# Expert layers of a two-block transformer: from gathering each token's experts to multiplying with all experts on TensorE

## The chip, the cores and the metric

The kernel runs on one core of a Trainium2 chip. The metric is the time of the device for one execution, in microseconds (us), as the median of several runs.

## What is computed

The program is two blocks on 256 tokens of width 1024. The change touches only `peer`, the expert layer. It is called three times on 256 tokens: in layer 0 for the latent tokens and for the context tokens, in layer 1 for the latent tokens.

```python
PEER_HEADS = 8; PEER_N_KEYS = 128; PEER_TOPK = 16        # 128 * 128 = 16384 experts
qry = (xb @ w_query).reshape(P, 8, 2, 128)
s = einsum('phcd,hckd->phck', qry, sub_keys)             # two scores of 128 keys for each head
top_s, top_i = top_k(s, 16)
cand_s = top_s[..., 0, :, None] + top_s[..., 1, None, :] # 256 candidates
best_s, pos = top_k(cand_s, 16)
idx = take_along_axis(top_i0 * 128 + top_i1, pos)        # 16 experts for each token and head
gate = softmax(best_s)
act = gelu(einsum('pd,phkd->phk', xb, u_tab[idx]))
return einsum('phk,phkd->pd', gate * act, v_tab[idx])
```

So each token takes 8 x 16 = 128 of 16384 experts. U and V have 16384 rows of 1024 numbers each, 67 MB a table and a layer in f32.

## The kernel before

The program is a list of stages (`Begin`, `Ada`, `DeltaNet`, `Peer` for layer 0, `Attention`, `Peer` for layer 1, and eight more). Each stage writes out one instruction list for each engine, and each engine starts a stage when all engines have ended the one before. SyncE (SP) alone runs ahead: it only issues loads into a ring of three buffers of 1 MB (`Ring.load`), and each load waits until the matmuls that read the block three loads earlier have ended.

`Peer` works on tiles of 128 tokens, four in layer 0 (stage `peer_a`) and two in layer 1 (`peer_m`). A tile's tokens lie on the 128 partitions. The steps are these.

- `NormFirst` normalizes the tiles and turns them into `hT`. `pe_step` projects queries and scores them against the keys, job by job.
- For each unit, a tile and a head, `dve_choose` picks the 16 experts of each token: MAX8, FIND_INDEX8 and MATCH_REPLACE8 over 128, 128 and 256 values, then a comparison with a row of numbers (`iota`) that turns positions into keys.
- For each of the unit's 16 experts per token, `pool_rows` (L1859) gathers by an indirect DMA one row of U and V together, 8 KB for each token, 1 MB for 128 tokens, into one of 8 buffers. A buffer is gathered into again when the matmul of 8 gathers before has ended.
- `dve_dot` (L1901) multiplies the U half with the token and sums it. ScalarE takes the gelu (L1794), `dve_coef` (L1913) multiplies with the gate, ScalarE makes a diagonal matrix of the 128 coefficients (L1801), and TensorE multiplies it with the V half into PSUM (`pe_sum`, L1766: two matmuls of 512 columns).

There are 32 units in layer 0 and 16 in layer 1, so 768 gathers of 1 MB, and as many rounds of these steps.

## Time and profile before

| | |
|---|---|
| time of three runs | 4365.11, 4366.67, 4370.96 us, median 4366.67 |
| span of the profiled execution | 4368.7 us |
| expert stage of layer 0 | 1196.8 to 2574.1 us |
| expert stage of layer 1 | 2724.5 to 3432.0 us |
| TensorE matmul busy over the span | 85% |
| VectorE, ScalarE, GpSimd busy | 58%, 22%, 28% |
| data moved | 1043.56 MB, mean 239 GB/s |

The profiled execution's own time is one of the three, which isn't named; the three lie from 3.6 us below to 2.3 us above its span. The span runs from the first instruction to the last. The stages follow one another on all engines, so the length of a stage adds to the time in full. Within a stage the engines overlap, and what counts is the step that the others wait for. TensorE's busy time holds waits inside its pipeline.

### The profile page before, as it was taken

What the parts mean: (1) busy time and instruction counts of PE and PEld (TensorE: products, weight loads), DVE (VectorE), ACT (ScalarE), POOL (GpSimd) and SP (SyncE); (2) the same over time, 40 slices, a digit from 0 to 9 for tenths busy, and PEclk for the clock granted to TensorE, in tenths of its full rate; (3) what the DMA queues carried; (4) which work ended last, traced back from release to release, by engine and by line L of the source; (5) the groups of instructions that cost most, each with busy time, mean ns of one, the idle gap of its engine ahead of it and who ended that gap; (6) DMA issues with size and microseconds to landing.
All of it is one profiled execution on the core that took longest, in us unless ns stands there. A gap on an engine that the chain in (4) does not pass through costs nothing.

```text
span 4368.7 us, 60065 instructions
## 1 busy us (share of the span) xinstructions
PE 3704.5 (85%) x23239; PEld 2027.7 (46%) x23239; DVE 2515.1 (58%) x5831; ACT 966.5 (22%) x2602; POOL 1218.9 (28%) x1241
## 2 busy tenths in 40 slices
PE   6898899888989987777777789888777789899999
PEld 2456744576444433222322235543222358546674
DVE  1345733567266777777777645767776347636341
ACT  0233312232132222222222212222222121010100
POOL 1004400243023444444444410344444100006000
PEclk7798999899999999999999999999999999999999
DMA  9410012100289999999999952999999524330443
GB/s 378 162 59 4 4 58 68 40 4 3 91 323 399 418 416 420 418 413 410 414 414 407 420 227 66 363 416 418 418 413 419 188 81 135 121 120 11 148 145 125
DMA packets 269482, 1043.56 MB, mean 239 GB/s; under 512 B 19394, under 2 KB 103596, under 8 KB 170896
## 3 DMA queue, kind: packets, MB, share of 16 engines
q0 software_dynamic: 114736, 815.52, 45.8%
q1 hardware_dynamic: 154464, 224.18, 15.3%
...
## 4 chain that ended last, share of the span: by engine, by line
PE 49%; DMA 27%; DVE 12%; ACT 4%; issue 4%; POOL 3%; DVEq 0%; POOLq 0%; ACTq 0%
DMA arena<-in_peer_uv,arena 25%; PE psum L261 13%; PE psum L1766 11%; PE psum L299 4%; PE psum L749 4%; PE psum L1724 3%; PE psum L788 3%; DVE arena L1901 2%; DMA arena<-in_ada_w 2%; PE psum L212 2%; POOL arena L1859 1%; PE psum L1091 1%; ACT arena L1801 1%; PE psum L1102 1%; DVE arena L946 1%
## 5 line engine op out<-in xcount | busy, mean ns | idle before, releaser
L1766 PE MATMUL psum<-arena 128*128 128x512 f32 x3072 | 1460.0, 620 | 392.4 <-ACT arena L1801 387.8
L1901 DVE SCALAR_TENSOR_TENSOR arena<-arena 128x1024 bf16<-128x1024 f32 x768 | 940.9, 1225 | 522.2 <-DMA arena<-in_peer_uv,arena 491.9
L1859 POOL DMA_INDIRECT arena<-in_peer_uv,arena x768 | 864.4, 1125 | 1174.1 <-PE psum L1766 1035.8
L1766 PEld LDWEIGHTS psum<-arena 128*128 128x128 f32 x3072 | 574.6, 196 | 1228.2 <-ACT arena L1801 636.8
L261 PE MATMUL psum<-ring,arena 128*128 128x512 f32 (+2 forms) x1408 | 593.1, 585 | 25.4 <-DVE arena L2780 9.1
L261 PEld LDWEIGHTS psum<-ring,arena 128*128 128x128 f32 x1408 | 269.3, 199 | 342.8 <-issue 316.5
L1794 ACT ACTIVATE arena<-arena 128x2 f32<-128x2 f32 x384 | 78.3, 204 | 1243.1 <-DVE arena L1901 1243.0
L1801 ACT ACTIVATE arena<-consts,arena 128x128 f32<-128x128 f32 x768 | 268.3, 394 | 224.6 <-DVE arena L1913 221.4
L299 PE MATMUL psum<-arena,ring 128*128 128x256 f32 x1408 | 309.6, 381 | 9.8 <-DVE arena L2775 7.7
L299 PEld LDWEIGHTS psum<-arena,ring 128*128 128x128 f32 x1408 | 267.3, 191 | 50.2 <-issue 6.4
L749 PE MATMUL psum<-arena,ring 128*128 128x512 f32 x512 | 230.4, 605 | 1.6 <-issue 1.6
L1724 PE MATMUL psum<-arena,ring 128*128 128x128 f32 (+3 forms) x704 | 181.7, 409 | 8.9 <-ACT arena L1539 8.9
L212 PE MATMUL psum<-consts,arena 128*128 128x128 f32 (+3 forms) x705 | 104.1, 290 | 67.3 <-DMA arena<-in_ev_b_spatial 19.1
L1724 PEld LDWEIGHTS psum<-arena,ring 128*128 128x128 f32 x704 | 119.7, 199 | 77.4 <-issue 49.5
L749 PEld LDWEIGHTS psum<-arena,ring 128*128 128x128 f32 x512 | 97.2, 195 | 113.8 <-issue 113.8
L212 PEld LDWEIGHTS psum<-consts,arena 128*128 128x128 f32 (+3 forms) x705 | 85.2, 149 | 115.2 <-issue 44.4
L2963 POOL TENSOR_TENSOR arena<-arena 128x512 f32<-128x512 f32 x32 | 40.6, 1269 | 331.2 <-DVE arena L2998 331.2
L330 ACT ACTIVATE arena<-x_res 128x1024 f32<-128x1024 f32 x10 | 10.6, 1060 | 486.0 <-DVE x_res L2787 322.0
L1298 POOL MEMSET arena<- 128x512 f32 x8 | 4.2, 522 | 391.8 <-ACT arena L902 391.7
L788 PE MATMUL psum<-ring,arena 128*128 128x512 f32 x256 | 110.4, 593 | 1.6 <-ACT arena L885 1.6
L1913 DVE SCALAR_TENSOR_TENSOR arena<-arena 128x2 f32<-128x2 f32 x384 | 81.1, 211 | 32.8 <-ACT arena L1794 31.4
L946 DVE SCALAR_TENSOR_TENSOR arena<-arena 128x512 f32<-128x512 f32 x128 | 96.2, 752 | 4.6
...
## 6 DMA issues: line engine op xcount, KB each, us to landing
arena<-in_ada_w SPq DMA_DIRECT2D x48, 1024.0 KB, 14.6
ring<-in_ffn_w_up SPq DMA_DIRECT2D x44, 1024.0 KB, 5.1
ring<-in_dn_w_in SPq DMA_DIRECT2D x24, 1024.0 KB, 5.3
ring<-in_peer_w_query SPq DMA_DIRECT2D x22, 1024.0 KB, 7.1
ring<-in_ffn_w_down SPq DMA_DIRECT2D x20, 1024.0 KB, 5.0
arena<-in_peer_uv,arena POOLq DMA_INDIRECT x768, 12.8
ring<-in_ev_w_in SPq DMA_DIRECT2D x10, 1024.0 KB, 5.2
ring<-in_dn_w_out SPq DMA_DIRECT2D x8, 1024.0 KB, 4.9
```

What stands on the lines that cost most here:

```text
L212: return e.transpose(out, in_, self.k.const("ident")[0:n, 0:n])
L261: m = e.matmul(o, self.hT[:, k0 + k, t * 128:(t + 1) * 128], w[:, k, :], start=k0 + k == 0, stop=k0 + k == self.KC - 1)
L299: m = e.matmul(self.bank(c)[:, 0:self.nt], w[:, k, j * 128:(j + 1) * 128], self.hT[:, k, 0:self.nt], start=k == 0, stop=k == self.KC - 1)
L749: m = e.matmul(k.banks[j % 4], w[:, q, j % 2 * 128:(j % 2 + 1) * 128], self.hT[:, q, :], start=q == 0, stop=q == 7)
L788: m = e.matmul(k.banks[t * 2 + nh], self.oT[:, k0 + q, t * 128:(t + 1) * 128], w[:, q, nh * 512:(nh + 1) * 512], start=k0 + q == 0, stop=k ...
L946: e.scalar_tensor_tensor(acc, p[:, :, w:w + 256], self.cw[:, c, w:w + 1], acc, MUL, ADD).then_inc(*V.up(("conv", half, j)))
L1724: m = e.matmul(k.banks[j % 2][:, 0:w_], w[:, n, c % 2 * 128:(c % 2 + 1) * 128], self.hT[:, n, a * 128:b * 128], start=n == 0, stop=n == 7)
L1766: m = e.matmul(k.banks[4 + t % 2 * 2 + nh], self.diag[g % self.ND], self.vsl[g % self.NS][:, nh * 512:(nh + 1) * 512], start=u % 8 == 0 an ...
L1801: e.activation(self.diag[g % self.ND], k.const("ident"), ACT.Copy, bias=0.0, scale=self.cf[u % 2][:, s:s + 1]).then_inc(*S.up(("dg", g)))
L1859: e.indirect_dma_start(self.uv[g % self.NS], None, self.table(), bass.IndirectOffsetOnAxis(ap=self.eid[u % 6][:, s:s + 1], axis=0)).then_i ...
L1901: e.scalar_tensor_tensor(self.junk[g % 2], self.us[g % self.NS], 1.0, self.h[:, u // 8, :], MUL, MUL, accum_out=self.a[u % 2][:, s:s + 1]) ...
L1913: e.scalar_tensor_tensor(self.cf[u % 2][:, c], self.lg[u % 4][:, c], self.sm[u % 4], self.ge[u % 2][:, c], MUL, MUL,).then_inc(*V.up(("cf" ...
```

## The change

The gathers are gone. Every expert is worked out for every token, and those that a token didn't choose get a gate of zero. 256 tokens (two tiles) make a half: layer 0 has two halves (`self.halves`), layer 1 has one. U and V are given in another layout (`peer_ut`, `peer_vt`), so that a load of 1 MB holds 256 experts, 8 KB for each partition, and lands in the ring of three buffers.

- `pe_u(n, c)`: chunk c of 128 experts, half n: 8 matmuls of 256 columns, experts on the partitions of PSUM and tokens in the columns. ScalarE's gelu puts the result into `Xs[:, c, :]`, which holds 128 chunks x 256 tokens for each partition, 128 KB.
- `pe_v(n, c)`: the same chunk's part of the output: 4 matmuls of 512 columns, with `Xs[:, c, :]` as weights.
- Order on TensorE: all of U of half 0 (128 chunks), then V of half n - 1 and U of half n chunk by chunk in turn (layer 0 only), then all of V of the last half.
- The gates: for a token, the 128 pairs (key 0, key 1) with their gates, turned so that pairs lie on partitions. A group is 4 tokens. VectorE compares keys with `iota` (`dve_group`, 128 x 1024), GpSimd multiplies one half with the gates (`pool_group`, 128 x 512, in place), TensorE multiplies the two (4 matmuls of 128 x 128), which gives the 128 x 128 gates of each of the 4 tokens. There are 64 groups for each half, and two buffers `hot`. They lie on TensorE in 66 slots behind the U chunks of a half (64 groups and two turns): chunks 60 to 120 of half 0 in layer 0, 76 to 120 in layer 1, 64 to 121 of half 1.
- ScalarE copies a group out of PSUM, and after each fourth writes 1 MB to DRAM (`G_d`, pieces of 512 bytes), from two buffers in turn: 16 writes a half. SP reads it back in 16 loads of 1 MB into one buffer `Gb`, one for 8 chunks. VectorE multiplies it into `Xs` (`dve_coef`, 128 x 2048), and `pe_v` of the 8 chunks waits for that.
- The choice of the experts (`dve_unit`, 16 for each half) stays, in one piece for each unit. `Norm` takes the place of `NormFirst`, and each query job is 8 matmuls over all tiles at once (`pe_query`, 16 jobs; `pe_score`).

The core of the diff:

```diff
+        self.Xs = flat.rearrange("p (c t) -> p c t", c=128)
+        self.stg = [res[:, 0:2048], res[:, 2048:4096] if nt > 2 else k.al(2048)]
+        self.Gb = hT[:, 0:2048]
+        self.hot = [k.al3(2, 4, 128) for _ in range(2)]
+        self.G_d = [k.nc.dram_tensor(f"coef_{name}_{n}", [16, 128, 256, 8], F32, kind="Internal").ap() for n in range(self.halves)]
...
+    def span(self, n):
+        if n:
+            return 64, 122
+        return (60, 121) if self.nt > 2 else (76, 121)
+    def slots(self, n, c):
+        a, b = self.span(n)
+        upto = lambda c: min(self.LAST, max(0, (c - a + 1) * self.LAST // (b - a)))
+        return range(upto(c - 1), upto(c)) if c else range(upto(0))
+    def exps(self, n):
+        if n:
+            return {30: 0, 60: 1}
+        return {20: 0, 58: 1} if self.nt > 2 else {34: 0, 72: 1}
...
 def sp(self, e):
...
+        for j in range(0, 16, 2):
+            load_block(k, e, self.query_key(j), k.i["peer_w_query"][l], 0, 8, j * 128, 256)
+        for b in range(64):
+            self.sp_rows(e, "u", 0, b)
+        for n in range(self.halves):
+            for b in range(64):
+                self.sp_rows(e, "v", n, b)
+                if b == 0:
+                    self.sp_coef(e, n, 0)
+                elif b % 4 == 1 and b < 60:
+                    self.sp_coef(e, n, b // 4 + 1)
+                if n + 1 < self.halves:
+                    self.sp_rows(e, "u", n + 1, b)
+    def sp_rows(self, e, kind, n, b):
+        table = self.k.i["peer_ut" if kind == "u" else "peer_vt"]
+        self.k.ring.load(e, (self.name, kind, n, b), lambda a: a, table[self.l, b])
+    def sp_coef(self, e, n, b):
+        if b == 0:
+            for s in (14, 15):
+                e.wait_ge(*self.l_put[s % 2].at(("put", n, s)))
+            e.wait_ge(*(self.V.at(("coef", n - 1, 15)) if n else self.P.at(("u", 0, 127))))
+        else:
+            e.wait_ge(*self.V.at(("coef", n, b - 1)))
+        e.dma_start(self.Gb, self.G_d[n][b].rearrange("j t i -> j (t i)")).then_inc(*self.l_got.up(("got", n, b)))
...
+        for n in range(self.halves + 1):
+            for c in range(128):
+                if n:
+                    self.pe_v(e, n - 1, c)
+                if n < self.halves:
+                    self.pe_u(e, n, c)
+                    for s in self.slots(n, c):
+                        self.pe_slot(e, n, s)
+    def pe_u(self, e, n, c):
+        ring, key = self.k.ring, self.u_key(n, c)
+        if c % 2 == 0:
+            e.wait_ge(*ring.ready(key))
+        if c >= 2:
+            e.wait_ge(*self.S.at(("ge", n, c - 2)))
+        elif n:
+            e.wait_ge(*self.S.at(("ge", n - 1, 126 + c)))
+        w = ring.buf(key).rearrange("p (c k m) -> p c k m", c=2, k=8)
+        for q in range(8):
+            m = e.matmul(self.k.banks[4 + c % 2][:, 0:256], w[:, c % 2, q, :], self.hT[:, n, q, :], start=q == 0, stop=q == 7)
+        m.then_inc(*self.P.up(("u", n, c)))
+        if c % 2:
+            ring.free(key, self.P)
+    def pe_v(self, e, n, c):
+        k, ring, key = self.k, self.k.ring, self.v_key(n, c)
+        if c % 2 == 0:
+            e.wait_ge(*ring.ready(key))
+        if c % 8 == 0:
+            e.wait_ge(*self.V.at(("coef", n, c // 8)))
+        if c == 0:
+            if n == 0:
+                e.wait_ge(*self.S.at(("sc", 15)))
+            else:
+                e.wait_ge(*self.S.at(("ge", n, 127)))
+                e.wait_ge(*self.S.at(("ev", n, 63)))
+        w = ring.buf(key).rearrange("p (c d) -> p c d", c=2)
+        for t in range(2):
+            for nh in range(2):
+                m = e.matmul(self.y_bank(n, t, nh), self.Xs[:, c, t * 128:(t + 1) * 128], w[:, c % 2, nh * 512:(nh + 1) * 512],
+                             start=c == 0, stop=c == 127)
+        m.then_inc(*self.P.up(("v", n, c)))
+        if c % 2:
+            ring.free(key, self.P)
...
+    def pe_slot(self, e, n, s):
+        P, b = self.P, self.slot_bank(s)
+        if s >= 2:
+            e.wait_ge(*self.taken(n, s - 2))
+        elif n:
+            e.wait_ge(*self.taken(n - 1, self.LAST - 2 + s))
+        if s in self.TURNS:
+            t = self.TURNS.index(s)
+            e.wait_ge(*self.V.at(("gate", n, t)))
+            for w in range(3):
+                m = self.turn(e, b[:, w * 128:(w + 1) * 128], self.PK[t][:, w, :])
+            m.then_inc(*P.up(("tp", n, t)))
             return
+        g = self.group(s)
+        e.wait_ge(*self.G.at(("gated", n, g)))
+        rows, cols = self.hot[g % 2][:, 1], self.hot[g % 2][:, 0]
+        for q in range(4):
+            m = e.matmul(b[:, q * 128:(q + 1) * 128], rows[:, q, :], cols[:, q, :], start=True, stop=True)
+        m.then_inc(*P.up(("g", n, g)))
...
+        if self.nt > 2:
+            e.wait_ge(*self.l_x.at("x"))
+        for n in range(self.halves):
+            for c in range(128):
+                if n == 0 and c == self.free_at[0]:
+                    e.wait_ge(*V.at(("picked", 0, 15)))
+                if n == 0 and c == self.free_at[1]:
+                    e.wait_ge(*self.l_sc.at("s"))
+                e.wait_ge(*P.at(("u", n, c)))
+                e.activation(self.Xs[:, c, :], k.banks[4 + c % 2][:, 0:256], ACT.Gelu, bias=0.0, scale=1.0).then_inc(*S.up(("ge", n, c)))
+                if c in self.exps(n):
+                    self.act_exp(e, n, self.exps(n)[c])
+                for s in self.slots(n, c):
+                    if s not in self.TURNS:
+                        self.act_group(e, n, self.group(s))
...
+    def act_group(self, e, n, g):
+        S, s = self.S, g // 4
+        lane, stg = self.l_put[s % 2], self.stg[s % 2].rearrange("p (b t i) -> p b t i", b=16, t=16)
+        if g % 4 == 0 and (s >= 2 or n):
+            e.wait_ge(*lane.at(("put", n, s - 2) if s >= 2 else ("put", n - 1, 14 + s)))
+        e.wait_ge(*self.P.at(("g", n, g)))
+        slot = g + 1 + (g > 1)
+        e.activation(stg[:, :, g % 4 * 4:g % 4 * 4 + 4, :].rearrange("p b t i -> p t b i"),
+                     self.slot_bank(slot).rearrange("p (t b i) -> p t b i", t=4, b=16), ACT.Copy, bias=0.0, scale=1.0).then_inc(*S.up(("ev", n, g)))
+        if g % 4 == 3:
+            e.wait_ge(*S.now())
+            e.dma_start(self.G_d[n][:, :, 16 * s:16 * s + 16, :].rearrange("b j t i -> j b (t i)"),
+                        stg.rearrange("p b t i -> p b (t i)")).then_inc(*lane.up(("put", n, s)))
...
+    def pool_group(self, e, n, g):
+        rows = self.hot[g % 2][:, 1]
+        e.wait_ge(*self.V.at(("hot", n, g)))
+        e.tensor_tensor(rows, rows, self.PT[g // 32][:, 2, g % 32 * 4:g % 32 * 4 + 4].unsqueeze(2).to_broadcast([128, 4, 128]),
+                        MUL).then_inc(*self.G.up(("gated", n, g)))
...
+        for u in range(16):
+            self.dve_unit(e, 0, u)
+        self.dve_first(e, 0)
+        for g in range(4, 64):
+            self.dve_group(e, 0, g)
+        for n in range(1, self.halves):
+            self.dve_coef(e, n - 1, 0)
+            for b in range(16):
+                if b < 15:
+                    self.dve_coef(e, n - 1, b + 1)
+                if b < 8:
+                    for u in (2 * b, 2 * b + 1):
+                        self.dve_unit(e, n, u)
+                else:
+                    if b == 8:
+                        self.dve_first(e, n)
+                    for g in range(max(4, 9 * (b - 8)), min(64, 9 * (b - 7))):
+                        self.dve_group(e, n, g)
+        last = self.halves - 1
+        for b in range(16):
+            self.dve_coef(e, last, b)
+            if b == 5:
+                for n in range(last):
+                    self.dve_add(e, n)
+        self.dve_add(e, last)
+    def dve_first(self, e, n):
+        self.dve_turned(e, n, 0)
+        self.dve_group(e, n, 0)
+        self.dve_group(e, n, 1)
+        self.dve_gates(e, n, 1)
+        self.dve_group(e, n, 2)
+        self.dve_group(e, n, 3)
+        self.dve_turned(e, n, 1)
...
+    def dve_group(self, e, n, g):
+        V, P = self.V, self.P
+        if g < 4 or g == 32:
...
+        e.tensor_tensor(self.hot[g % 2], self.k.const("iota").unsqueeze(1).unsqueeze(1).to_broadcast([128, 2, 4, 128]),
+                        self.PT[g // 32][:, 0:2, g % 32 * 4:g % 32 * 4 + 4].unsqueeze(3).to_broadcast([128, 2, 4, 128]),
+                        ALU.is_equal).then_inc(*V.up(("hot", n, g)))
+    def dve_coef(self, e, n, b):
+        e.wait_ge(*self.l_got.at(("got", n, b)))
+        e.wait_ge(*self.S.at(("ge", n, 8 * b + 7)))
+        x = self.Xs[:, 8 * b:8 * b + 8, :]
+        e.tensor_tensor(x, x, self.Gb.rearrange("p (t i) -> p i t", i=8), MUL).then_inc(*self.V.up(("coef", n, b)))
...
-    given["peer_uv"] = np.concatenate([given.pop("peer_u"), given.pop("peer_v")], axis=2)
+    u = given.pop("peer_u").reshape(2, 64, 2, 128, 8, 128).transpose(0, 1, 5, 2, 4, 3)
+    given["peer_ut"] = np.ascontiguousarray(u).reshape(2, 64, 128, 2048)
+    v = given.pop("peer_v").reshape(2, 64, 2, 128, 1024).transpose(0, 1, 3, 2, 4)
+    given["peer_vt"] = np.ascontiguousarray(v).reshape(2, 64, 128, 2048)
```

On TensorE, in the middle of a tile of layer 0, the order before was: two matmuls for a gather (its buffer's name is uv0, uv1, ...), each pair with a wait for the gather and for ScalarE, and projection steps between.

```order
L1766 MATMUL psum<-arena 128x512 [waits uv0_peer_a_landed,act_peer_a]
L1766 MATMUL psum<-arena 128x512
L1766 MATMUL psum<-arena 128x512 [waits uv1_peer_a_landed,act_peer_a]
L1766 MATMUL psum<-arena 128x512
L212 MATMUL psum<-consts,arena 128x128 x8
L1766 MATMUL psum<-arena 128x512 [waits uv2_peer_a_landed,act_peer_a]
L1766 MATMUL psum<-arena 128x512
L1724 MATMUL psum<-arena,ring 128x512 [waits act_peer_a,ring0_landed]
L1724 MATMUL psum<-arena,ring 128x512 x3
L1766 MATMUL psum<-arena 128x512 [waits uv3_peer_a_landed,act_peer_a]
L1766 MATMUL psum<-arena 128x512
L1766 MATMUL psum<-arena 128x512 [waits uv4_peer_a_landed,act_peer_a]
```

At the start of the stretch where both halves are worked on, TensorE's order now is this: L1721 is V of half 0, L1701 is U of half 1, and the ring's three buffers are named in the waits.

```order
L1721 MATMUL psum<-ring,arena 128x512 [waits act_peer_a,dve_peer_a,ring2_landed]
L1721 MATMUL psum<-ring,arena 128x512 x3
L1701 MATMUL psum<-arena,ring 128x256 [waits act_peer_a,ring0_landed]
L1701 MATMUL psum<-arena,ring 128x256 x7
L1721 MATMUL psum<-ring,arena 128x512 x4
L1701 MATMUL psum<-arena,ring 128x256 [waits act_peer_a]
L1701 MATMUL psum<-arena,ring 128x256 x7
L1721 MATMUL psum<-ring,arena 128x512 [waits ring1_landed]
L1721 MATMUL psum<-ring,arena 128x512 x3
L1701 MATMUL psum<-arena,ring 128x256 [waits act_peer_a,ring2_landed]
L1701 MATMUL psum<-arena,ring 128x256 x7
L1721 MATMUL psum<-ring,arena 128x512 x4
```

The waits for 768 gathers are gone, and a wait for one of three ring buffers stands ahead of every second V and every second U chunk. The U block of two chunks takes the buffer of the V block of the two chunks before (ring2 here), and that V block is in use until its last matmul.

On SP's queue the loads of layer 0 before were these: the queries, a row of gates for the end, and the next stage's weights.

```order
L104 DMA ring<-in_peer_w_query 128x8x256 [waits pe_dn] x2
L104 DMA ring<-in_peer_w_query 128x8x256 [waits pe_peer_a] x10
L1671 DMA arena<-gates_d 128x1024 [waits dve_peer_a]
L104 DMA ring<-in_att_w_in 128x4x512 [waits pe_peer_a] x3
L104 DMA ring<-in_att_w_in 128x4x512 [waits pe_att] x3
```

Now the same queue holds the U and V blocks, and the loads of the gates (L1632) among them.

```order
L104 DMA ring<-in_peer_w_query 128x8x256 [waits pe_peer_a] x6
L104 DMA ring<-in_peer_ut 128x2048 [waits pe_peer_a] x64
L104 DMA ring<-in_peer_vt 128x2048 [waits pe_peer_a]
L1632 DMA arena<-coef_peer_a 128x2048 [waits pe_peer_a,coef_out1_peer_a_landed,coef_out0_peer_a_landed]
L104 DMA ring<-in_peer_ut 128x2048 [waits pe_peer_a]
L104 DMA ring<-in_peer_vt 128x2048 [waits pe_peer_a]
L1632 DMA arena<-coef_peer_a 128x2048 [waits dve_peer_a]
L104 DMA ring<-in_peer_ut 128x2048 [waits pe_peer_a]
L104 DMA ring<-in_peer_vt 128x2048 [waits pe_peer_a]
L104 DMA ring<-in_peer_ut 128x2048 [waits pe_peer_a]
L104 DMA ring<-in_peer_vt 128x2048 [waits pe_peer_a]
L104 DMA ring<-in_peer_ut 128x2048 [waits pe_peer_a]
```

64 U blocks stand behind the queries, then V and U in turn, and each load of the gates waits for VectorE's multiplication of the one before.

## Rows read from the trace of the kernel before

**Rows 1.** The page: chain by line; a group, busy | idle before.

```profile
DMA arena<-in_peer_uv,arena 25%; PE psum L261 13%; PE psum L1766 11%; PE psum L299 4%; PE psum L749 4%; PE psum L1724 3%; PE psum L788 3%; DVE arena L1901 2%; DMA arena<-in_ada_w 2%; PE psum L212 2%; POOL arena L1859 1%; PE psum L1091 1%; ACT arena L1801 1%; PE psum L1102 1%; DVE arena L946 1%
...
L1766 PE MATMUL psum<-arena 128*128 128x512 f32 x3072 | 1460.0, 620 | 392.4 <-ACT arena L1801 387.8
```

**Rows 2.** Busy time by stretch: expert stages, then an FFN.

```profile
core 0: us, PE busy (x) PEld busy (x) DVE busy (x) ACT busy (x) POOL busy (x), PEclk, DMA share, GB/s
1196.80:1277.00 80.20, 60.60 (x300) 42.65 (x301) 53.16 (x158) 30.86 (x83) 20.02 (x18) 0.87 0.81 288
1277.00:2571.00 1294.00, 1040.77 (x2366) 434.64 (x2364) 915.28 (x2272) 326.06 (x904) 554.42 (x495) 0.98 1.00 410
2724.50:2767.00 42.50, 34.28 (x216) 30.59 (x216) 26.90 (x94) 17.25 (x41) 8.17 (x9) 0.96 0.80 289
2767.00:3429.00 662.00, 527.73 (x1264) 230.97 (x1264) 459.36 (x1139) 161.70 (x467) 282.83 (x248) 0.97 0.99 407
4090.00:4242.00 152.00, 151.99 (x704) 133.79 (x704) 73.94 (x151) 9.94 (x23) 0.00 (x0) 1.00 0.45 146
```

**Rows 3.** The chain in order of time: start us, length us.

```profile
632.69 55.22 PE psum L788 x128
1203.79 3.82 PE psum L1724 x32
4090.01 152.20 PE psum L299 x704
```

**Rows 4.** Loads: issues, size, median us from issue to landing.

```profile
ring<-in_ffn_w_up SPq DMA_DIRECT2D x44, 1024.0 KB, 5.1
ring<-in_peer_w_query SPq DMA_DIRECT2D x22, 1024.0 KB, 7.1
ring<-in_peer_sub_keys SPq DMA_DIRECT2D x2, 0.5 KB, 6.3
```

**Rows 5.** The loads of in_ffn_w_down, 20 of 24 with 1 MB.

```profile
DMA to landing us min/median/max: 3.5/5.0/5.5
```

**Rows 6.** Timeline of SP at 4104 us: start, length of the issue.

```profile
4104.10 0.37 SPq L104 DMA_DIRECT2D ring<-in_ffn_w_up  x1
```

**Rows 7.** Timeline of VectorE: starts of two units of the choice.

```profile
1208.80 0.30 DVE L1932 MAX8 arena<-arena 128x8 f32<-128x128 f32 x1 [3.25 <-ACT arena L1829]
...
1218.22 0.30 DVE L1932 MAX8 arena<-arena 128x8 f32<-128x128 f32 x1
```

**Rows 8.** Groups by shape on VectorE.

```profile
L955 DVE TENSOR_TENSOR arena<-arena 128x1024 f32<-128x1024 f32 x8 | 9.8, 1226 | 0.3
```

**Rows 9.** The page: a group on GpSimd.

```profile
L2963 POOL TENSOR_TENSOR arena<-arena 128x512 f32<-128x512 f32 x32 | 40.6, 1269 | 331.2 <-DVE arena L2998 331.2
```

**Rows 10.** Timeline of VectorE and GpSimd from 499.2 us.

```profile
499.20 0.82 POOL L1319 TENSOR_TENSOR arena<-arena 128x384 f32<-128x384 f32 x1
...
499.99 1.26 POOL L1321 TENSOR_TENSOR arena<-arena,consts 128x512 f32<-128x512 f32 x1
...
500.49 1.18 DVE L1448 TENSOR_TENSOR arena<-arena 128x384 f32<-128x384 f32 x1
...
501.21 1.13 POOL L1319 TENSOR_TENSOR arena<-arena 128x384 f32<-128x384 f32 x1
...
505.27 0.52 DVE L1448 TENSOR_TENSOR arena<-arena 128x384 f32<-128x384 f32 x1
```

**Rows 11.** Timeline of TensorE behind layer 0's experts.

```profile
2574.12 5.36 PE L212 MATMUL psum<-consts 128*128 128x128 f32 x24 [3.00 <-issue]
...
2587.36 5.13 PE L261 MATMUL psum<-ring,arena 128*128 128x512 f32 x8 [1.51 <-ACT arena L340]
```

**Rows 12.** Timeline: norm of four tiles, start and what follows.

```profile
146.16 1.06 ACT L330 ACTIVATE arena<-x_res 128x1024 f32<-128x1024 f32 x1 [124.25 <-DVE arena L572]
...
159.69 5.57 PE L261 MATMUL psum<-ring,arena 128*128 128x64 f32 x25 [0.84 <-ACT arena L340]
```

**Rows 13.** Timeline: norm of two tiles, its start.

```profile
4082.91 1.06 ACT L330 ACTIVATE arena<-x_res 128x1024 f32<-128x1024 f32 x1 [1.53 <-DVE x_res L3019]
```

539 lines of the change are left out of this document (177 added, 362 removed).

## Prediction

> **What bounds the kernel now.** I start with the stages. The two expert stages last 1377.3 us (1196.8 to 2574.1) and 707.5 us (2724.5 to 3432.0), 2084.8 of a span of 4368.7. Beside them only the loads that SP issues ahead of the next stage move, so the answer is the new length of these two. Next the busy times by stretch [rows 2]: in both stretches of gathers the DMA engines are busy for a share of 0.99 to 1.00 and move 407 to 410 GB/s. At that rate 1 MB (1.049 million bytes) takes 2.56 us, and 768 of them 1965. The chain agrees [rows 1]: 25% of it are gathers; TensorE's 11% in L1766 stand between them because a buffer comes free with its matmul. So DMA is the bound.
>
> How much of TensorE is in use there is the next question, and the busy row can't tell: 1041 of 1294 us hold waits inside the pipeline.
>
> **The price of a matmul.** It must be taken for each instruction of the program, not for each record. The kernel issues two matmuls for each of 768 gathers, 1536, and the page counts 3072 [rows 1]: a matmul in f32 leaves two records. An FFN layer shows the same: 22 blocks of 1 MB (44 loads for two layers [rows 4]), 16 matmuls each, are 352, and the chain counts 704 in 152.20 us [rows 3]. So:
> - 256 columns: 152.20 / 352 = 0.432 us. This is the very shape of U, from the same ring, with no stop.
> - 512 columns: 55.22 / 64 = 0.863 us, the shape of V (L788, 128 records).
> - 128 columns: 3.82 / 16 = 0.239 us. A turn leaves one record, 0.119.
>
> A U chunk is 8 x 0.432 = 3.46 us, a V chunk 4 x 0.863 = 3.45, a group of gates 4 x 0.239 = 0.955. TensorE's real work for the gathers before was 1536 x 0.863 = 1326 us of 1956, under the DMA's bound.
>
> The Trainium skill has two figures here. FP8 and Floating Point Precision, TensorE Precision Notes, says that true FP32 takes 4 passes through the array; Perfetto Trace Analysis, Engine Utilization, halves the peak output rate for FP32_LOW_HIGH. The trace sides with the first: 0.863 us for 512 columns are 2070 cycles at 2.4 GHz, 4.04 a column; the second fits only a single record. By the first the sum is as below, by the second TensorE's share of it is half (rival 3).
>
> **What the change removes.** All 1965 us of gathers, 768 sums on VectorE and as many diagonals. **What it adds:** three passes over U and V. On TensorE 3 x 128 x (3.46 + 3.45) = 2653 us, and 192 groups, 183. On DMA 3 x 128 loads of 1 MB, 48 writes and 48 reads of gates: 480 x 2.56 = 1229 us, or 1300 if the writes in 512-byte pieces cost 4.1 each (below). TensorE has more than twice the DMA's work, and more than the stages last now. It becomes the bound, if the others keep ahead of it.
>
> **Layer 0, step by step.**
> - Norm of four tiles: 13.5 us from its start to the next projection [rows 12].
> - Queries: 16 jobs of 8 x 0.863 + 4 x 0.239 = 7.86 us, 125.7. One us for the last score's copy, and 2 for a slow clock: behind a gap 8 records of 512 columns took 5.13 us, against 3.45 [rows 11, 3].
> - U of half 0: 128 x 3.46 = 442.8, 64 groups 61.1, turns 0.7: 504.6.
> - Turn to V: the first gates are loaded only behind the last U matmul, since `Gb` lies in `hT`. 0.25 us to SP's issue (two blocks from 4090.01 end at 4103.85 [rows 3], the issue is at 4104.10 [rows 6]), about 4.8 for the load (5.0 is the median [rows 5]; pieces of 8 KB instead of 2 and 4, so 0.2 off, an estimate), and a product of 128 x 2048, twice 1.23 [rows 8]: 7.5, with TensorE idle. Then the slow clock: 24 turns took 5.36 us, against 2.9 [rows 11]; 3 us. Sum 10.5.
> - V of half 0 and U of half 1: 128 x 6.91 = 884.5, groups 61.8: 946.3.
> - V of half 1: 441.7 and 0.8 for the last gelu: 442.5.
> - The sums at the end: 3.6 us as before.
>
> Sum: 13.5 + 128.7 + 504.6 + 10.5 + 946.3 + 442.5 + 3.6 = 2049.7, against 1377.3: **672.4 us more**.
>
> **Layer 1.** Norm of two tiles 8 (7.1 from 4082.91 to 4090.01 [rows 13, 3], and the keys' turns ahead), queries 16 x (3.46 + 0.48) + 1 = 64, U 504.6, turn 10.5, V 441.7, end 3.6. Sum 1032.4 against 707.5: **324.9 us more**.
>
> Together 997.3, and the span goes to 5366. The profiled execution lies 2 us over the median: **5364 us**.
>
> **What hides the rest, and with what margin.**
> - *The ring.* In the stretches of one kind a block lasts 6.92 us, and a load has two blocks' time. The thin place is the mixed stretch: the U block of 2b, 2b+1 goes into the buffer of the V block of 2b-2, 2b-1, free after V(2b-1). Until U(2b) TensorE has U(2b-1) and V(2b), 6.91 us, and the load takes 0.25 + 4.8 = 5.05. Without that cover each us of lateness costs 64. At 7.1, the landing of query blocks beside gathers [rows 4], it is 0.44 x 64 = 28 us.
> - *The groups.* The comparison takes 1.23 us [rows 8], the multiplication 1.27 [rows 9], and they don't overlap [rows 10]: VectorE's product of 128 x 384, 0.52 us alone, took 1.18 when it began at 500.49, and ended 0.42 behind GpSimd's (501.25); GpSimd's next took 1.13 behind it, not 0.82. So a group needs 2.5 us. TensorE asks for one each 4.1 us in layer 0 ((61 x 3.46 + 62) / 66), 3.3 in layer 1 (45 chunks), 7.0 in the mixed stretch (58). With no cover 64 x 2.5 would stand in each half, 480 in all.
> - *VectorE's choice.* A unit takes 9.4 us [rows 7], 16 take 151, and the first groups come 208 us (layer 0) and 263 us (layer 1) into U, behind 128 and 64 us of queries. The eleventh unit waits for an exponential that ScalarE issues at chunk 20 or 34 (69 and 118 us into U); six units behind it are 56 us, still in time. In the mixed stretch two units and a product are 21 us for 8 chunks of 55.
> - *The gates' writes.* A write takes some 4.1 us of DMA: 1 MB in 512-byte pieces lands after 6.3 us [rows 4], 1.5 over my 4.8. Four groups, its period, are 13 us or more. VectorE holds groups back at each eighth chunk of the mixed stretch, waiting for the next gates (about 7 us, then 2.5), but TensorE needs the first of them only 14.8 us in.
> - *ScalarE* has a gelu and a copy for each chunk, about 1 us of 3.46.
>
> **The unknown costs, from both sides.** Ring: 0 or 28. Turns, two of them: with a landing of 3.5 and no slow clock 4.3 less each, with 7.1 and twice the slow clock 5.3 more each; 10 either way. Groups: if the multiplication with its broadcast took twice as long, the pair needs 3.8 us, over layer 1's 3.3: 66 x 0.5 = 33 more. Writes: none of this kind stands in the trace. Free, nothing changes; at twice the price, 8.2, a period of 13 us still holds one and two loads (13.3), so nothing but some lateness changes; at thrice, 12.3, it lacks 4.4 us, 16 x 4.4 = 70 more in layer 1. Slots: 200 changes of shape on TensorE, nothing or 0.1 us each, 20. Clock: granted 1.00 in the FFN's 152 us, 0.98 in the gathers [rows 2]; at 0.98 throughout it is 2% of 3082, 60 more.
>
> **The rivals.**
> 1. *Slower still: TensorE is kept waiting.* Landings of 7.1, groups at 3.8, the clock at 0.98: 28 + 33 + 60, so 5390 to 5485. For it: such dense work for 2000 us isn't in the trace. Against it: the FFN asked the same ring for a block each 6.92 us, as the new stretches do, and ran without a stop. Chance 0.2.
> 2. *The gates' traffic stops ScalarE.* Gelus stand behind a copy that waits for a write; 48 writes each 10 us over their period would give 480 more, 5844. It begins at a write of 13 us in layer 1 and 16 in layer 0. Chance 0.04.
> 3. *Not slower: an f32 matmul costs one record.* If in these shapes the two records overlapped, a chunk were 1.73 us. TensorE's 3025 us of work in the stages (2653 + 183 + 189 of queries) halve, 1512 less; the ring then lacks 5.05 - 3.46 = 1.6 us for each pair in the mixed stretch, 102, and the pair of VectorE and GpSimd sets the pace of the groups, 25 and 53: 5366 - 1512 + 180 = 4034. It would have to hold for new instructions of just the shapes that cost two records in L299 and L788. The case turns when 997 of the 3025 go, at 67% of the rows' price. Chance 0.02.
> 4. *Somewhat less:* a V chunk uses each weight tile for two matmuls in a row, and the turns may be short: 10 to 35 us less, 5330 to 5350. Chance 0.06.
>
> **How the numbers follow.** My forecast, 5350 to 5390, has 0.66; the first rival 0.2, the second 0.04, the third 0.02, the fourth 0.06, and 0.02 for what I don't see, with either sign. The range of 5330 to 5460 takes in most of the first and the fourth. A measurement of this kernel can tell about 0.2%. Slower 0.97, same 0.005, faster 0.025.
>
> **What would show it.** TensorE's busy share in the new stages near 1 and its clock at 1.00; in the page 6144 records for U, 3072 for V and 1536 for groups; V alone at 3.45 us a chunk, a ring load that lands in 5 us and waits for TensorE, DMA share under 0.5, GpSimd's multiplications a chunk apart, two idle times of 7.5 us ahead of the first V. The prediction is wrong if the chain names DMA, ScalarE or GpSimd in these stages for more than some 30 us, or if a U chunk takes anything but 3.46.

## The result and the profile after

The changed kernel takes **5348.24 us** (median; 5345.55 to 5349.44) beside 4365.89 (4363.11 to 4370.96) for the kernel before on the same chip: a ratio of 1.224, with a 95% interval of 1.2226 to 1.2261. 5364 was forecast. The profiled execution has a span of 5347.5 us at a mean clock of 0.971.

The page, the chain by line and five groups (busy, mean ns | idle before, releaser), which answer to [rows 1]:

```profile
PE 84%; DVE 7%; ACT 3%; issue 3%; DMA 2%; POOL 2%; DVEq 0%; SPq 0%; POOLq 0%; ACTq 0%
PE psum L1721 25%; PE psum L1701 25%; PE psum L261 11%; PE psum L299 4%; PE psum L1757 3%; PE psum L1673 3%; PE psum L752 3%; PE psum L791 2%; DMA arena<-in_ada_w 2%; PE psum L212 1%; PE psum L1094 1%; PE psum L1105 1%; DVE arena L949 1%; POOL arena L2979 1%; POOL arena L2980 1%
...
L1701 PE MATMUL psum<-arena,ring 128*128 128x256 f32 x6144 | 1364.9, 379 | 0.0
L1721 PE MATMUL psum<-ring,arena 128*128 128x512 f32 x3072 | 1344.6, 594 | 18.4 <-issue 17.7
...
L1924 DVE TENSOR_TENSOR arena<-arena 128x2048 f32<-128x2048 f32 x48 | 186.3, 3881 | 1075.3 <-DMA arena<-coef_peer_a 644.0
...
L1915 DVE TENSOR_TENSOR arena<-consts,arena 128x1024 f32<-128x1024 f32 x192 | 232.3, 1224 | 603.9 <-PE psum L1757 603.8
L1851 POOL TENSOR_TENSOR arena<-arena 128x512 f32<-128x512 f32 x192 | 228.6, 1197 | 1426.2 <-DVE arena L1915 1426.2
```

TensorE now holds 84% of the chain, and U (L1701) and V (L1721) a quarter of the span each. In front of the 3072 matmuls of U TensorE never waited; in front of V 18.4 us, nearly all of it the two turns. The other engines wait for it or for each other: VectorE's comparison (L1915) for TensorE, GpSimd (L1851) for VectorE. In the page's list of loads the ring keeps pace:

```profile
ring<-in_peer_ut SPq DMA_DIRECT2D x192, 1024.0 KB, 4.8
ring<-in_peer_vt SPq DMA_DIRECT2D x192, 1024.0 KB, 4.8
...
coef_peer_a<-x_res ACTq DMA_DIRECT2D x32, 1024.0 KB, 5.8
arena<-coef_peer_a SPq DMA_DIRECT2D x32, 1024.0 KB, 6.9
```

Busy time by stretch of the changed kernel, layer 0 and then layer 1 (queries, U, turn, mixed, V), answers to [rows 2]:

```profile
1209.80:1335.80 126.00, 126.00 (x385) 63.85 (x386) 59.72 (x232) 18.62 (x32) 0.00 (x0) 0.99 0.19 60
1335.80:1836.40 500.60, 500.11 (x2566) 446.43 (x2565) 158.58 (x371) 94.50 (x199) 72.09 (x66) 1.00 0.50 170
1836.40:1845.30 8.90, 0.00 (x0) 0.01 (x1) 3.84 (x1) 0.38 (x1) 0.00 (x0) 0.76 0.87 345
1845.30:2789.80 944.50, 942.73 (x3590) 642.34 (x3590) 278.44 (x616) 92.99 (x198) 81.78 (x80) 1.00 0.51 179
2789.80:3229.60 439.80, 439.70 (x1024) 194.48 (x1024) 63.76 (x24) 0.00 (x0) 1.53 (x3) 1.00 0.53 196
...
3454.30:3954.70 500.40, 499.91 (x2567) 446.67 (x2566) 168.78 (x415) 94.32 (x199) 84.57 (x65) 1.00 0.50 167
3954.70:3963.90 9.20, 0.40 (x2) 0.03 (x1) 3.84 (x1) 0.38 (x1) 0.00 (x0) 0.64 0.59 228
3963.90:4408.00 444.10, 441.48 (x1024) 195.12 (x1024) 60.70 (x19) 0.00 (x0) 0.00 (x0) 1.00 0.52 188
```

The first figure behind the length is TensorE's busy time: 500.11 of 500.60, 942.73 of 944.50, 439.70 of 439.80, with a granted clock of 1.00. DMA, at 0.99 to 1.00 in the stretches of gathers before, is down at 0.50 to 0.53 in these long stretches. The bound moved from DMA to TensorE, whose work is simply longer. Layer 0's stage lasts 2039.3 us (1377.3 before), layer 1's 1027.9 (707.5): 982.4 more together, and the span grew by 978.8.

The timeline of the first turn shows what a turn is made of:

```profile
1834.73 1.67 PE L1701 MATMUL psum<-arena,ring 128*128 128x256 f32 x7
...
1836.50 0.33 SPq L1632 DMA_DIRECT2D arena<-coef_peer_a  x1
...
1841.38 3.84 DVE L1924 TENSOR_TENSOR arena<-arena 128x2048 f32<-128x2048 f32 x1 [33.13 <-DMA arena<-coef_peer_a]
...
1845.32 5.46 PE L1721 MATMUL psum<-ring,arena 128*128 128x512 f32 x6 [8.92 <-issue]
```

U's last matmul ends at 1836.40, the gates' load is issued 0.10 us later and has landed at 1841.38, the product takes 3.84, and V starts at 1845.32. Its first records are slow, as in [rows 11]: the chain has 6.60 us for 8 of them, where 4 x 0.863 = 3.45 is the full clock's price, and the granted clock is 0.50 from 1845.3 to 1851.0. Layer 1's turn is shorter in this part: 8.81 us idle, a granted clock of 0.50 only from 3963.9 to 3967.0, and 441.5 us for V where half 1 of layer 0 took 439.7 without a gap ahead of it.

### The profile page after: what moved, and what is told of

Its sections match the earlier page's. It is cut to its first block, busy times and chain, and to the rows that moved or that the text cites. A ratio compares the mean times of both kernels' runs of the same rounds, so it can differ in the third digit from the quotient of the medians.

```text
span 5347.5 us, 70742 instructions
## 1 busy us (share of the span) xinstructions
PE 5062.9 (95%) x30697; PEld 3344.0 (63%) x30697; DVE 1926.4 (36%) x4079; ACT 760.9 (14%) x1806; POOL 594.6 (11%) x685
## 4 chain that ended last, share of the span: by engine, by line
PE 84%; DVE 7%; ACT 3%; issue 3%; DMA 2%; POOL 2%; DVEq 0%; SPq 0%; POOLq 0%; ACTq 0%
PE psum L1721 25%; PE psum L1701 25%; PE psum L261 11%; PE psum L299 4%; PE psum L1757 3%; PE psum L1673 3%; PE psum L752 3%; PE psum L791 2%; DMA arena<-in_ada_w 2%; PE psum L212 1%; PE psum L1094 1%; PE psum L1105 1%; DVE arena L949 1%; POOL arena L2979 1%; POOL arena L2980 1%
## 5 line engine op out<-in xcount | busy, mean ns | idle before, releaser
L1701 PE MATMUL psum<-arena,ring 128*128 128x256 f32 x6144 | 1364.9, 379 | 0.0
L1721 PE MATMUL psum<-ring,arena 128*128 128x512 f32 x3072 | 1344.6, 594 | 18.4 <-issue 17.7
L1701 PEld LDWEIGHTS psum<-arena,ring 128*128 128x128 f32 x6144 | 1159.1, 190 | 207.9 <-issue 61.4
L1721 PEld LDWEIGHTS psum<-ring,arena 128*128 128x128 f32 x3072 | 580.8, 191 | 698.4 <-issue 694.8
L1924 DVE TENSOR_TENSOR arena<-arena 128x2048 f32<-128x2048 f32 x48 | 186.3, 3881 | 1075.3 <-DMA arena<-coef_peer_a 644.0
L261 PEld LDWEIGHTS psum<-ring,arena 128*128 128x128 f32 x1408 | 267.5, 198 | 342.3 <-issue 315.7
L1915 DVE TENSOR_TENSOR arena<-consts,arena 128x1024 f32<-128x1024 f32 x192 | 232.3, 1224 | 603.9 <-PE psum L1757 603.8
L1851 POOL TENSOR_TENSOR arena<-arena 128x512 f32<-128x512 f32 x192 | 228.6, 1197 | 1426.2 <-DVE arena L1915 1426.2
L299 PE MATMUL psum<-arena,ring 128*128 128x256 f32 x1408 | 310.0, 381 | 9.8 <-DVE arena L2791 7.7
L299 PEld LDWEIGHTS psum<-arena,ring 128*128 128x128 f32 x1408 | 267.1, 191 | 50.6 <-issue 6.4
L1757 PEld LDWEIGHTS psum<-arena 128*128 128x128 f32 x1536 | 196.2, 192 | 11.3 <-POOL arena L1851 1.8
L1757 PE MATMUL psum<-arena 128*128 128x128 f32 x1536 | 197.4, 275 | 2.1 <-POOL arena L1851 2.1
L1673 PE MATMUL psum<-arena,ring 128*128 128x512 f32 (+1 forms) x512 | 171.8, 489 | 3.4 <-ACT arena L343 1.9
L752 PEld LDWEIGHTS psum<-arena,ring 128*128 128x128 f32 x512 | 96.3, 193 | 112.6 <-issue 112.6
L1673 PEld LDWEIGHTS psum<-arena,ring 128*128 128x128 f32 x512 | 95.6, 192 | 64.8 <-issue 55.0
L791 PE MATMUL psum<-ring,arena 128*128 128x512 f32 x256 | 110.4, 593 | 1.6 <-ACT arena L888 1.6
```

What stands on the lines that cost most here:

```text
L261: m = e.matmul(o, self.hT[:, k0 + k, t * 128:(t + 1) * 128], w[:, k, :], start=k0 + k == 0, stop=k0 + k == self.KC - 1)
L299: m = e.matmul(self.bank(c)[:, 0:self.nt], w[:, k, j * 128:(j + 1) * 128], self.hT[:, k, 0:self.nt], start=k == 0, stop=k == self.KC - 1)
L752: m = e.matmul(k.banks[j % 4], w[:, q, j % 2 * 128:(j % 2 + 1) * 128], self.hT[:, q, :], start=q == 0, stop=q == 7)
L791: m = e.matmul(k.banks[t * 2 + nh], self.oT[:, k0 + q, t * 128:(t + 1) * 128], w[:, q, nh * 512:(nh + 1) * 512], start=k0 + q == 0, stop=k ...
L1673: m = e.matmul(o, w[:, q, j % 2 * 128:(j % 2 + 1) * 128], self.hT[:, :, q, :], start=q == 0, stop=q == 7)
L1701: m = e.matmul(self.k.banks[4 + c % 2][:, 0:256], w[:, c % 2, q, :], self.hT[:, n, q, :], start=q == 0, stop=q == 7)
```

## The experiments

The theory of the prediction: the two f32 matmul loops set the time, each at the price of its rows, and all else is hidden with the margins named. Its rivals: the ring or DMA sets it, the gates' chain of VectorE and GpSimd, or an f32 matmul is not to be reckoned at two records. The first four kernels take half of U's matmuls away, double the loads, and cut the passes of a matmul, in the changed kernel and in the one before. A time with a ratio beside it, and that of the doubled comparisons, is the median of four or five runs; each of the others is a single run.

**Half of U's matmuls.** The sum over the features runs over 4 of 8 tiles; the rest of U's product is left out.

```diff
-        for q in range(8):
+        for q in range(4):
...
```

> Leaves out the second four of the eight matmuls of each U chunk, so the gelus see half a dot product; loads, gates, V and all waits stay. 3 x 128 x 4 = 1536 matmuls of 256 columns go. If TensorE's time is the price of its matmuls, they are worth 1536 x 0.432 = 664 us and the time is 4685 us, perhaps 10 more, since in layer 1 a slot then comes each 2.1 us and the comparison and multiplication of a group take 2.3. If loads or the path of the gates had a part in the bound, less than 600 us go.

Measured: 4751.42 us, 597 less and not 664. That is just under the 600 that I had named as the mark of loads or gates in the bound, so this run by itself doesn't settle it. V alone stayed at 440.1 and 442.1 us. U alone fell from 500 to 307 us in layer 1, where 4 x 128 x 0.432 = 221 less were due, and the mixed stretch from 944 to 744 (221 due, 201 got). The page has a part of the rest:

```profile
L1701 PE MATMUL psum<-arena,ring 128*128 128x256 f32 x3072 | 712.6, 383 | 12.6 <-DMA ring<-in_peer_ut 11.3
...
L1757 PE MATMUL psum<-arena 128*128 128x128 f32 x1536 | 204.2, 278 | 25.2 <-POOL arena L1851 25.2
```

U waits for its loads for the first time, and the gates' matmuls 25 us for GpSimd: 38 of the 67 us. Most of the others lie in TensorE's busy time, which is 25 us over what was due in these three stretches, at a granted clock of 0.98 to 0.99 and not 1.00. With the whole of U the same two waits were 0.0 and 2.1 us. So TensorE is the bound of the changed kernel, and at half of U's work the next ones begin.

**Every block loaded twice**, the second load behind the first one's landing; nothing is left out.

```diff
...
+        e.wait_ge(*ring.ready(key))
+        e.dma_start(ring.buf(key), table[self.l, b]).then_inc(*ring.landed[ring.slot[key]].up(key))
```

> Each U and V block is loaded twice in a row into its buffer, the second load issued when the first has landed. The loads' bytes double and a block lands about 9.85 us after its buffer came free instead of 5.05. If TensorE is the bound and loads are hidden: no change in the stretches of U or of V alone (13.8 us of slack), and in the mixed stretch 9.85 - 6.91 = 2.9 us late for each of 64 pairs of chunks, 190 us: 5540. If bytes were the bound, 384 more loads of 2.56 us would cost 980.

Measured: 5767.91 us, 420 more: more than double what I expected, and under half of what bytes would ask. U alone grew by 12 us (layer 0) and 19, V alone by 76 and 61, the mixed stretch by 250. The stretches of one kind were to stay as they were: they have 168 of the 420. Its busy row shows that bandwidth isn't what ran out (share 0.70, 254 GB/s), while DMA now holds 36% of the chain:

```profile
PE 50%; DMA 36%; DVE 6%; ACT 3%; issue 3%; POOL 1%; SPq 1%; DVEq 0%; POOLq 0%; ACTq 0%
...
1852.90:3047.70 1194.80, 1014.68 (x3590) 676.72 (x3590) 276.05 (x616) 92.63 (x197) 86.80 (x79) 0.94 0.70 254
```

A block came each 1194.8 / 128 = 9.3 us. I had reckoned with the delay of a block by itself, and not with SP, which stands at its wait while the next block's buffer is already free. SP's own waits in the mixed stretch agree: 734 of its 1195 us pass at the wait of a second load for the first, 354 at a buffer. No run tests this reading by itself. What the run does show: 384 MB more through the same queues cost 420 us, where 384 x 2.56 = 983 would be owed to a kernel bound by bytes.

**The upper halves only, in the changed kernel.** U's and V's matmuls read the upper 16 bits of both operands as bf16; the lower 16 bits are left out of these two products. Loads and instruction counts stay.

```diff
+def high(a):
+    return a.bitcast(BF16).rearrange("p (n two) -> p n two", two=2)[:, :, 1]
...
-            m = e.matmul(self.k.banks[4 + c % 2][:, 0:256], w[:, c % 2, q, :], self.hT[:, n, q, :], start=q == 0, stop=q == 7)
+            m = e.matmul(self.k.banks[4 + c % 2][:, 0:256], high(w[:, c % 2, q, :]), high(self.hT[:, n, q, :]), start=q == 0, stop=q == 7)
...
```

> U and V matmuls read only the upper 16 bits of each number of their two operands, as bf16 with a step of two; nothing else changes. The values lose precision (they are cut to bf16). One record instead of two, and a quarter of the time: U and V chunks of 0.87 us. TensorE's work falls by 3/4 of 2640 us, 1980. If price times count of f32 matmuls is what made the change slower, the time falls below that of the kernel before, to what the next limits allow: in U alone the loads at 2.6 us a block and the groups at 2.3 each, in the mixed stretch 5.05 + 1.73 us a pair and the slots, in V alone 2.56 x 1.25 a block. Sum about 1650 us for the two stages instead of 3067: 3950 us, 3850 to 4150. If TensorE's price isn't the reason, the time stays over 4366.

**The same cut in the kernel before**, in its sum over the gathered rows of V.

> The kernel before with the same cut in its matmuls of the gathered V rows (upper 16 bits of the coefficients and of V). 1536 matmuls of 512 columns fall from 0.863 to about 0.215 us, 995 us of TensorE's work. The gathers are its bound, so at most a few per cent go, where a buffer came free with a matmul: 4366 to 4250 us. If TensorE had a larger part in the bound before than I read, more.

Measured: the changed kernel 4089.31 us, 0.9366 of the kernel before (0.935 to 0.9381); the kernel before, cut alike, 4356.55 us, 0.9967 (0.9953 to 0.9981). The same cut takes 1259 us from one and 11 to 14 from the other (by the medians or by the ratio). In the latter the gathers hold 33% of the chain, as DMA's bound asks, and TensorE's granted clock in the stretches of gathers fell from 0.98 to 0.57 without making the kernel longer. In the former loads take TensorE's place; the last row is V alone of layer 0:

```profile
L1705 PE MATMUL psum<-arena,ring 128*128 128x256 bf16 x3072 | 441.7, 294 | 264.0 <-DMA ring<-in_peer_ut 255.4
...
ring<-in_peer_ut SPq DMA_DIRECT2D x192, 1024.0 KB, 6.4
ring<-in_peer_vt SPq DMA_DIRECT2D x192, 1024.0 KB, 7.8
...
2194.60:2426.10 231.50, 146.14 (x504) 51.45 (x512) 67.43 (x24) 0.39 (x1) 1.63 (x3) 0.86 0.93 371
```

U has 3072 records for 3072 matmuls, where f32 left 6144. The mixed stretch took 597 us, where 64 pairs at 6.78 and the groups come to some 491, so I undervalued the ring's round trip there.

In most places a cut chunk waits for its load, and its price can't be seen. In the kernel with seven buffers and late groups (below) TensorE ran twelve chunks without a stop, at a granted clock of 1.00:

```profile
1596.42 1.06 PE L1739 MATMUL psum<-ring,arena 128*128 128x512 bf16 x4
1597.32 1.08 PE L1718 MATMUL psum<-arena,ring 128*128 128x256 bf16 x8
1598.24 1.06 PE L1739 MATMUL psum<-arena 128*128 128x512 bf16 x4
```

From start to start a V chunk is 0.90 us and a U chunk 0.91 to 0.92, against 3.44 and 3.46 in f32: 3.8 times less.

**U's matmuls alone, V's alone.** Each reads the upper halves in one loop only; the lower halves are left out there.

> The changed kernel; only the 3072 matmuls over U read the upper 16 bits of both operands (the lower halves are left out), V stays f32. Theory (TensorE pays by the row's price, 0.432 us a U matmul, until loads set the pace): a U chunk falls from 3.46 to 0.87 us, so the two stretches of U alone go to the pace of the loads that the kernel with both cuts showed (269 and 259 us instead of 510 each), and the mixed stretch to about 650 of 944, since a block then needs 6.89 + 1.73 + 0.9 us on TensorE for two loads and the ring's slack of 4.3 us is under a landing of 5. Sum 787 less: 4560 us (4500 to 4650). If loads cost nothing, 997 less, 4351. Rival (U's matmuls were not what set the time, V's were): under 300 less, over 5050.

> The changed kernel; only the 1536 matmuls over V read the upper 16 bits of both operands, U stays f32. Theory: a V chunk falls from 3.45 to 0.87 us; V alone goes to 231 and 217 us instead of 440 each, the mixed stretch to about 650 of 944, U alone stays at 500. Sum 727 less: 4621 us (4560 to 4700). In both this run and the one with U cut, TensorE saves the same work (997 us by the rows), so the two must lie within some 100 us of each other. Rival (a 512-column matmul is bound by something else than the passes, such as its weight load): V alone stays over 350, and the time over 4850.

Measured: 4613.98 and 4648.86 us, 734 and 699 less, and 35 apart. With U cut, V alone is untouched (443 us); with V cut, so is U alone (509.5 us with the turn, as in the changed kernel). Both mixed stretches came to 679 and 675 us, 25 to 30 over what I expected. So each loop is on the path by itself, and the work of each weighs the same.

**Where the time of the cut kernel goes.** First the gelus in bf16, in place as before, which frees 8 MB.

```diff
-        self.Xs = flat.rearrange("p (c t) -> p c t", c=128)
+        self.Xs = flat[:, 0:16384].bitcast(BF16).rearrange("p (c t) -> p c t", c=128)
```

> The changed kernel with the upper 16 bits in U and V (4089 us), and the gelus, multiplied by the gates in place, held in bf16 instead of f32; the lower halves are left out as there. It is the control for the next kernel, which needs the room that this frees. Theory: the loads set the pace, so 4089 again (4070 to 4110); the product on VectorE stays at 3.9 us, if it is the stride in the gates' buffer that makes it slow, and falls below 3 if it is the traffic of 128 x 2048 f32 on both sides.

Measured: 4093.87 us, and 3.85 us a product: nothing moved. Then four more buffers in that room, the groups of gates and the exponentials earlier, and the loads of the gates two blocks later in SP's queue:

```diff
...
+    def ring_of(self, key):
+        return self.k.ring if self.place[key] % 7 < 3 else self.deep
...
-        return (60, 121) if self.nt > 2 else (76, 121)
+        return (26, 121) if self.nt > 2 else (66, 121)
```

> The kernel with bf16 gelus, and in the room that they free four more 1 MB buffers: blocks of U and V take turns through seven instead of three, and the groups of gates begin earlier (chunk 26 instead of 60 in layer 0, 66 instead of 76 in layer 1). Theory (in the kernel with the upper halves each load waits for a buffer, so it is the landing of 4 to 8 us over three buffers that sets 4.06 us a block, not the 2.56 us of 1 MB at 410 GB/s): the mixed stretch falls from 597 to 460 us, V alone from 231 and 217 to 180 each, U alone from 269 to 240 and from 259 to 253, where 64 groups at 2.3 to 2.6 us behind 16 units of VectorE become the bound. Sum 250 less: 3840 us (3780 to 3920), DMA share over 0.85 in the stretches with V. Rival (DMA itself is the limit at 4 us a block, because the gates' writes and reads and several loads share it): 4089, same within 30.

Measured: 3990.58 us, a ratio of 0.9134 (0.9115 to 0.9152): 99 less and not 250. The gain is in the mixed stretch (511 us) and in V alone (205.5 and 193.8), but U of layer 0, with its turn, took 309 us instead of 269. In the waits of that stretch, two rows point to the cause:

```profile
ACT x_res L1827 <- DMA coef_peer_a<-x_res: 55.5, 9, 9.6
ACT arena L1817 <- DVE arena L2007: 44.1, 1, 44.1
```

My schedule had put ScalarE's exponential where VectorE's choice was 44 us from done, and its copies of the groups waited nine times for a write. The gelus, and so TensorE, stood behind both: TensorE waited 83 us for gelus, 45 of them at once. V alone had a simpler reason, a slip in my sum: 64 blocks and 16 MB of gates are 80 x 2.56 = 205 us, not 180.

The next two kernels put layer 0's groups back to chunk 60 and its exponentials to 20 and 58, and then gave the gates that are read back two buffers, in the place of the scores. In the latter the first loads of gates don't wait for U's last matmul any more:

```diff
-        self.Gb = hT[:, 0:2048]
+        self.Gb = [flat[:, 28672 + n * 2048 - (4096 if nt > 2 else 0):][:, 0:2048] for n in range(2)]
...
```

> The kernel with seven buffers, but layer 0's groups of gates begin at chunk 60 again, and its exponentials stand at chunks 20 and 58. In the kernel with seven buffers (3990) U alone took 309 us in layer 0, 40 more than with three: ScalarE, and behind it the gelus and TensorE, waited 44 us for VectorE's selection at the exponential of chunk 24, and 55 us for the gates' writes. Theory (it was where I put the exponential): U alone comes back to 255 (240 to 270), the time to 3935 (3920 to 3950). Rival (the writes, which land in 15 us beside seven loads, stop ScalarE wherever the groups stand): U alone stays near 300 and the time near 3990.

> The same, and the gates that are read back get two buffers of 128 x 2048 in the place of the scores instead of one, so that the next 1 MB lands while VectorE multiplies. With one buffer, 16 loads of 8.6 us and 16 products of 3.84 stand one behind the other in each stretch of V, 199 us, and the stretches took 205 and 194 us; but DMA was busy there for 1.00 of the time as well, 80 MB at 2.56 us are 205. Theory (DMA's bandwidth is the bound in V alone): these stretches stay at 190 to 205, the mixed one falls from 511 to 480, and the time is 3905 us (3880 to 3935). Rival (the round trip through the one buffer is the bound): V alone falls to 170 in both layers as well, and the time to 3850.

Measured: 3936.32 us with U of layer 0 at 266.7 (255 expected); the wait at the exponential is gone and that for writes is down to 19.3 us, and since both were moved at once, their shares are not told apart. Then 3874.92 us, a ratio of 0.8882 (0.8867 to 0.8897). The last is the fastest kernel of this study. Its busy rows for mixed, V of layer 0, V of layer 1:

```profile
1599.30:2042.20 442.90, 332.90 (x2053) 219.59 (x2054) 286.85 (x615) 90.73 (x197) 100.91 (x79) 0.88 0.94 370
2042.20:2245.50 203.30, 141.62 (x515) 50.25 (x512) 67.10 (x24) 0.39 (x1) 1.63 (x3) 0.87 1.01 421
...
2736.10:2925.90 189.80, 140.15 (x511) 49.64 (x512) 57.91 (x15) 0.00 (x0) 0.00 (x0) 0.90 1.01 420
```

V alone stayed (203 and 190), at a DMA share of 1.01: there it is the bytes (190 us at 420 GB/s are 76 of layer 1's 80 MB; I take it that the others landed before), and the one gate buffer was not the bound. The mixed stretch fell by 63 us, twice what I expected, to within 2% of its bytes: 128 blocks at 2.56 and 16 writes and reads at 4.1 and 2.56 are 434 us, the 4.1 for a write being the estimate of the prediction.

**The comparisons twice, in the changed kernel in f32.** Each of the 192 is issued twice into the same place.

```diff
+        for name in (None, ("hot", n, g)):
...
```

> The changed kernel, and each of the 192 comparisons of VectorE is issued twice into the same buffer, the second behind the first. It tests the cover of the groups: VectorE and GpSimd then need 2 x 1.22 + 1.04 = 3.5 us a group. Theory (TensorE is the bound and asks for a group each 3.9 us in layer 0, 7 in the mixed stretch, 3.2 in layer 1 by the measured chunk and group): nothing in layer 0, and 66 x 0.25 = 16 us in layer 1; 5348 + 16 = 5364 us (5350 to 5385). Rival (the comparisons stand on the path, one behind the other): 192 x 1.22 = 234 more, 5582.

Measured: 5371.18 us, 23 more. U of layer 1 went from 500.4 to 517.1, the 16 us that were worked out; layer 0's U grew by 4.5 and the mixed stretch by 0.8. VectorE's wait for TensorE in layer 1's U, 127.4 us in the changed kernel, is down to 35.2:

```profile
DVE arena L1916 <- PE psum L1757: 35.2, 42, 1.9
```

234 us of work were added and 23 reached the path.

**The gates read in a row.** The gates go to the wrong gelus; the amount of work stays.

```diff
-        e.tensor_tensor(x, x, self.Gb.rearrange("p (t i) -> p i t", i=8), MUL).then_inc(*self.V.up(("coef", n, b)))
+        e.tensor_tensor(x, x, self.Gb.rearrange("p (i t) -> p i t", i=8), MUL).then_inc(*self.V.up(("coef", n, b)))
```

> The changed kernel, but VectorE's product reads the gates one behind the other in the buffer and not each eighth value, so that the gates go to the wrong gelus; the work is the same. The term in question is the product at the turn, that I put at 2.45 us and that took 3.88. Theory (the stride of 32 bytes in the second operand makes it slow): a product takes 2.4 us (2.2 to 2.7), each of the two turns is 1.4 us shorter, and the time stays within 0.1%: 5345 us, since TensorE waits for a product only there. Rival (an operation of 128 x 2048 with two f32 operands in memory takes 3.9 in any order): 3.8 to 3.9, nothing changes.

Measured: 5343.31 us in one run, and a group of 2.29 us a product:

```profile
L1924 DVE TENSOR_TENSOR arena<-arena 128x2048 f32<-128x2048 f32 x48 | 110.0, 2293 | 1135.2 <-DMA arena<-coef_peer_a 643.1
```

The stride costs 1.6 us. TensorE's idle time at the two turns went from 8.92 and 8.81 us to 7.30 and 7.42. 48 x 1.6 = 76 us of VectorE's time went away, and these 3 us are what TensorE got of it; the single time can't resolve them, the trace can.

## Why the prediction was right

**The bound.** "It becomes the bound, if the others keep ahead of it": shown. TensorE's share of the chain is 84%, and in layer 0's stage the loads of gates have 0.3% of it and GpSimd's multiplication 0.2%; half of U's matmuls take 597 us away; either loop, cut to its upper halves, takes about 700; and 983 us worth of additional loads cost 420. Of the signs that the prediction named one failed by a little: the DMA share is 0.50 to 0.53, not under 0.5.

**The price of a matmul.** This step carried the number, and it was right. 384 chunks of each kind were reckoned at 3.46 and 3.45 us. Measured: V alone 439.7 / 128 = 3.44, and the mixed stretch, 128 of both with 64 groups, 944.5 against 946.3. That two records belong to one f32 instruction is shown once more by the bf16 runs, with one record each. The chunks of 0.90 us that bf16 needs agree with a nearly fourfold price. By the Trainium skill (FP8 and Floating Point Precision, TensorE Precision Notes) true FP32 needs 4 passes through the array; this trace agrees, since V alone took 439.7 / 512 = 0.859 us a matmul, 4.03 cycles a column at 2.4 GHz. Rival 3 would have needed a chunk of 1.73 us and is out.

**The terms**, predicted and measured, in us:

| | predicted | measured |
|---|---|---|
| norm, four tiles | 13.5 | 13.6 |
| queries of layer 0, with the wait behind the norm | 128.7 | 126.0 |
| U of half 0 | 504.6 | 500.6 |
| turn of layer 0: idle, then slow clock | 7.5 + 3 | 8.9 + 3.1 |
| turn of layer 1 | 7.5 + 3 | 8.8 + 1.8 |
| mixed, without the slow clock | 946.3 | 941.4 |
| V of half 1 | 442.5 | 439.8 |
| the sums at the end | 3.6 | 5.8 |
| layer 0's stage | 2049.7 | 2039.3 |
| layer 1's stage | 1032.4 | 1027.9 |

- *A group of gates was mis-sized*: put at 0.955, it took (500.6 - 442.8 - 0.7) / 64 = 0.89 in U. 192 x 0.065 = 12 us of the 16 by which I was too high. The price came from [rows 3], 3.82 us for 32 records just behind an idle time; where the engine was busy before, the same 32 took 3.59 us in the kernel before too (at 1240.06 us), 0.224 an instruction. The 0.1 us for a change of shape that I held possible don't show.
- *The product was mis-sized*: 3.88 us, not 2.45. I had doubled the row of a contiguous operation of half the size, and the operand is read with a stride of 32 bytes. It cost 1.4 at each turn, where the load took 4.98 us from U's end to the product instead of 5.05, and nothing between the turns.
- *The end*: eight operations on VectorE take 5.5 us, where I had copied 3.6 from before.
- *The slow clock behind a gap* cost 3.1 us in layer 0, as forecast, and 1.8 in layer 1; the granted clock was 1.00 over all long stretches. The 60 us for a clock of 0.98 were not needed.
- *Rival 4 has the number, not the mechanism.* 5348 lies in its 5330 to 5350 and 2 us under the bracket of my own forecast, 5350 to 5390. But the turns were longer than forecast, and V's weight tiles gave 2 us at most in each stretch of V alone; it is the groups that made the time lower. The terms too high and those too low partly cancel, so the sum is nearer than its parts allow: some of that is luck.

**What hides the rest.** The ring: landings of 4.8 us, and no idle time ahead of U. The groups: the pair was put at 2.5 us; it is 2.26, as GpSimd's part takes 1.04 (median) instead of 1.27, and doubling the comparison used up the margin in layer 1 at just the point that the sum gave (3.5 against 3.24). The writes landed in 5.8 us, of the 13 at which they would begin to hurt in layer 1. (The 6.3 us in [rows 4] that stood for them are those of a load of 1 MB; the 0.5 KB of that row is one of its pieces.) Rivals 1 and 2 are thus out for this kernel. They came alive once TensorE was quick: GpSimd's groups, the writes and the ring all appear among the waits of the kernels in bf16.
